# The first modulation's quarters on TensorE in the order first, third, second, fourth, and earlier loads of the next layer's scale quarters

## What is computed

```
mod = silu(c) @ w_ada[i] + b_ada[i]             # 1024 x 3072
sh, sc, gt = split(mod, 3)                      # shift, scale, gate: 1024 each
u = rms_norm(h, norm_g[i]) * (1 + sc) + sh
h = h + gt * mixer(u)
```

## Time and profile before

| | us |
|---|---|
| median of 3 runs | 1441.58 (1438.05 to 1445.44) |
| profiled execution | 1439.64 |
| its span | 1437.8 |
| TensorE busy | 1387.0 (96%) |
| VectorE busy | 749.6 (52%) |
| ACT, POOL busy | 578.9, 501.3 |
| mean granted TensorE clock | 0.972 of full |

### The profile page before, as it was taken

One profiled execution on the slowest core, in us unless ns is written; L12 is line 12 of the kernel. 1 busy time (PEld: TensorE's weight loads), 2 busy tenths in 40 slices (PEclk: granted clock), 3 DMA queues, 4 the chain that ended last, 5 costly groups with the idle time before them and its releaser, 6 DMA issues.

```text
span 1437.8 us, 18275 instructions
## 1 busy us (share of the span) xinstructions
PE 1387.0 (96%) x6981; PEld 1154.2 (80%) x6981; DVE 749.6 (52%) x1007; ACT 578.9 (40%) x892; POOL 501.3 (35%) x235
## 2 busy tenths in 40 slices
PE   7999999979999999999999999999999999999998
PEld 4688788769888888877879779788888888888886
DVE  3695888744845438477345425441635335253442
ACT  3444565514433344455444434443334223142331
POOL 0242000136531584311234213224475444444441
PEclk9999999989999999999999889989999999999999
DMA  9862001157322143211223113113333333333331
GB/s 344 270 216 68 3 19 30 30 174 231 97 76 57 57 133 103 74 44 45 76 60 88 45 44 88 44 51 96 102 88 103 89 102 95 95 102 88 101 97 65
DMA packets 204503, 136.20 MB, mean 95 GB/s; under 512 B 7033, under 2 KB 185834, under 8 KB 204442
## 3 DMA queue, kind: packets, MB, share of 16 engines
q1 hardware_dynamic: 204240, 135.32, 31.1%
q10 hardware_dynamic: 202, 0.06, 0.0%
HBM read 130.64 MB, written 4.72 MB: 94 GB/s over the span
## 4 chain that ended last, share of the span: by engine, by line
PE 83%; DVE 9%; ACT 3%; DMA 2%; issue 1%; POOL 1%; SPq 0%; ACTq 0%; DVEq 0%; POOLq 0%
PE psum L1972 26%; PE psum L1974 25%; PE psum L1973 25%; DMA ada_w<-in_w_ada 1%; PE psum L2020 1%; DVE pt_lo L1498 1%; PE psum L2169 1%; DMA ada_back<-in_w_ada 1%; DVE neg_max L1505 1%; POOL w_lo L642 1%; DVE psum L1448 1%; ACT w_hi L752 1%; PE psum L2410 1%; DVE probs L1493 1%; ACT pt_hi L898 1%
## 5 line engine op out<-in xcount | busy, mean ns | idle before, releaser
L642 POOL TENSOR_TENSOR w_lo<-w_raw,w_hi 128x1024 fp32r<-128x1024 f32 x180 | 439.7, 2446 | 745.6 <-ACT w_hi L752 617.5
L1972 PE MATMUL psum<-u_hi,w_hi 128*128 128x512 f32 (+1 forms) x960 | 373.3, 389 | 3.5 <-ACT decay_sum L1178 2.5
L1973 PE MATMUL psum<-u_lo,w_hi 128*128 128x512 f32 (+1 forms) x960 | 364.4, 380 | 0.0
L1974 PE MATMUL psum<-u_hi,w_lo 128*128 128x512 f32 (+1 forms) x960 | 364.1, 379 | 0.0
L752 ACT ACTIVATE w_hi<-w_raw 128x1024 fp32r<-128x1024 f32 x180 | 189.1, 1055 | 189.3 <-PE psum L1974 155.7
L1972 PEld LDWEIGHTS psum<-u_hi,w_hi 128*128 128x128 f32 x960 | 184.5, 192 | 42.9 <-issue 6.4
L1974 PEld LDWEIGHTS psum<-u_hi,w_lo 128*128 128x128 f32 x960 | 183.7, 191 | 34.0
L1973 PEld LDWEIGHTS psum<-u_lo,w_hi 128*128 128x128 f32 x960 | 184.3, 192 | 32.7 <-issue 1.4
L1972 PE MATMUL psum<-y_hi,w_hi 128*128 128x512 f32 x416 | 162.4, 390 | 0.0
L1973 PE MATMUL psum<-y_lo,w_hi 128*128 128x512 f32 x416 | 161.9, 389 | 0.0
L1974 PE MATMUL psum<-y_hi,w_lo 128*128 128x512 f32 x416 | 161.8, 389 | 0.0
(11 more groups left out here) (439 smaller groups left out, 2368.9 us busy)
## 6 DMA issues: line engine op xcount, KB each, us to landing
w_raw<-in_w_in SPq DMA_DIRECT2D x52, 512.0 KB, 3.8
ada_back<-in_w_ada SPq DMA_DIRECT2D x8, 2048.0 KB, 12.0
w_raw<-in_w_up SPq DMA_DIRECT2D x32, 512.0 KB, 4.0
w_raw<-in_w_down SPq DMA_DIRECT2D x32, 512.0 KB, 4.0
ada_w<-in_w_ada SPq DMA_DIRECT2D x4, 2048.0 KB, 14.8
w_raw<-in_fno_w_in SPq DMA_DIRECT2D x16, 512.0 KB, 3.7
w_raw<-in_mla_w_in SPq DMA_DIRECT2D x11, 512.0 KB, 4.8
w_raw<-in_mla_w_out SPq DMA_DIRECT2D x8, 512.0 KB, 4.1
```

The lines of the kernel that those rows point to most:

```text
L642: pool.tensor_tensor(WL[:, j, :], RAW[:, j % 2, :], f(WH[:, j, :]), ALU.subtract).then_inc(lo_done, 1)
L1972: pe.matmul(out, ah, bh, start=first, stop=False)
L1973: pe.matmul(out, ah, bl, start=False, stop=False)
L1974: return pe.matmul(out, al, bh, start=False, stop=last)
```

## The change

The four first quarters all go through TensorE, in the order 0, 2, 1, 3; their loads are queued as 0, 2, then the small bias tables, then 1, 3. VectorE's weighing of quarter 1, the selecting matmuls and eight warming matmuls go. The rstd diagonals and their matmuls come directly behind `ada(0)`. ACT splits weight tiles A0 0 and 1 behind the third row copy instead of behind the second. The fourth quarter's row is started behind `u0_lo` 3, since it shares a PSUM bank with a chunk of u.

Of the later quarters, r = 4 gets a buffer of its own (`AL4`, over the attention's finished latents); SyncE loads it once the last head's last scores are done, ahead of MO tile 4. Load 5 waits for the last weighing of values instead of the split output; load 6 follows MO tile 5 with no wait of its own, load 7 waits for `modulation(5)`. VectorE does `modulation(4)` in three pieces around the last head's end, and `modulation(5)` in two, behind output tiles 0 and 1. TensorE's sums of both move between half tiles 1 and 2.

```diff
+        AROW += [at("ada_row2", 166, [2, T]), at("ada_row3", 204, [2, T])]
+        AL4 = at("ada_late", 168, [P, KC, T])
...
-        ADA0 = 5
+        ADA0 = 6
-            return bank(2 if q == 3 else 6)
+            return bank(6 if q in (0, 3) else 2)
-            return AD[0] if r == 0 else AB[(r + 1) % 2]
+            return AD[0] if r == 0 else AL4 if r == 4 else AB[(r + 1) % 2]
@@ SyncE
             sp.dma_start(AQ[0][:], ada_weights(0)).then_inc(s_adaq[0], 16)
+            sp.dma_start(AQ[2][:], ada_weights(2)).then_inc(s_adaq[2], 16)
             sp.dma_start(T5[:], d["t5_bias_2"]).then_inc(s_t5, 16)
...
-            for q in range(1, 4):
+            for q in (1, 3):
                 sp.dma_start(AQ[q][:], ada_weights(q)).then_inc(s_adaq[q], 16)
...
-            for j in range(6):
+            for j in range(4):
                 out_tile(j)
-            sp.wait_ge(o_lo, HEADS)
+            sp.wait_ge(s_mm, 4 * HEADS)
             gate_load(4)
+            out_tile(4)
+            sp.wait_ge(un_mm, unit_mm_no(LAST, O_LAT))
             gate_load(5)
+            out_tile(5)
+            gate_load(6)
             out_tile(6)
             out_tile(7)
...
-            for r in range(6, 8):
-                sp.wait_ge(ada_used, r)
-                gate_load(r)
+            sp.wait_ge(ada_used, 6)
+            gate_load(7)
@@ ACT
             ada_row_copy(1, 2, 2)
-            split_hi(A0, None, 0)
-            split_hi(A0, None, 1)
...
             for c in range(4):
                 lat_hi(c)
-            ada_row_copy(2, 3, 4)
+            ada_row_copy(2, 1, 4)
+            split_hi(A0, None, 0)
+            split_hi(A0, None, 1)
+            ada_row_copy(3, 3, 5)
@@ VectorE
-            weigh_quarter(0)
             v.wait_ge(row_ss, TT + 1)
...
-            weigh_quarter(1).then_inc(ada_used, 1)
...
+            modulation(4, 0, 4)
             unit(LAST, O_LAT)
+            modulation(4, 4, 7)
             output(LAST)
             output_lo(LAST)
+            modulation(4, 7)
...
                 attention_added(c, bank(c), slice(0, T))
                 if c < 2:
-                    modulation(4 + c)
+                    modulation(5, 4 * c, 4 * c + 4)
@@ TensorE
+            pe.wait_ge(x_copied, KC)
             ada(0)
-            pe.wait_ge(bias_row, 1)
-            pe.wait_ge(x_copied, KC)
...
-            turn_row(0, 0)
-            for _ in range(8):
-                pe.matmul(bank(3, P), ONES[:], ONES[:], start=True, stop=True)
-            ada(2)
             pe.wait_ge(diag_done, TT)
...
+            turn_row(0, 0)
+            ada(2)
+            pe.wait_ge(bias_row, 1)
+            pe.matmul(bank(0), T5R[:], HOT[:, 0:T], start=True, stop=True)
+            pe.matmul(bank(1, P), T5R[:], HOT[:, T:TOEP], start=True, stop=True).then_inc(bias_mm, 1)
+            turn_row(1, 2).then_inc(ada_mm, 1)
+            ada(1)
+            pe.wait_ge(u0_lo, 3)
             ada(3, 0, 1)
-            turn_row(1, 2).then_inc(ada_mm, 1)
+            turn_row(2, 1)
             ada(3, 1, KC)
             def last_columns():
-                turn_row(2, 3)
...
+                turn_row(3, 3).then_inc(ada_mm, 1)
...
-            modulation(4)
-            modulation(5)
             for j in range(4):
                 pe.wait_ge(lo_done, MO + 4 + j + 1)
                 half_tile(0, j, j).then_inc(mo_half, 1)
+                if j == 1:
+                    modulation(4)
+                    modulation(5)
```

More of the change, by code:

```diff
@@ L190, in build @@
         DIAG = at("rstd_diag", 160, [P, TT, P])
-        SEL = at("two_columns", 155.875, [P, 2, 2])
         AROW = [at(f"ada_row{n}", 164 - 2 * n, [2, T]) for n in range(2)]
-        AROW.append(at("ada_row2", 166, [2, T]))
+        AROW += [at("ada_row2", 166, [2, T]), at("ada_row3", 204, [2, T])]
         XTOK = at("x_tok", 104, [P, TT, D])
@@ L544, in _ @@
             gate_tile(4)
-            sp.wait_ge(ada_used, 3)
+            sp.wait_ge(ada_used, 2)
             gate_load(3)
@@ L848, in head_hi @@
                 act.activation(WH[:, h % 4, 0:768], RAW[:, h % 2, 0:768], ACT.Copy).then_inc(hi_done, 1)
-            act.wait_ge(ada_used, 2)
+            act.wait_ge(ada_used, 1)
             for r in range(7):
@@ L1334, in _ @@
             v.memset(RSC[:], 0.0).then_inc(ones_set, 1)
-            link(v.memset(SEL[:], 1.0))
-            link(v.memset(SEL[:, 0, 1:2], 0.0))
-            v.memset(SEL[:, 1, 0:1], 0.0).then_inc(ones_set, 1)
             v.wait_ge(cols_t, 1)
@@ L1363, in _ @@
                 v.tensor_scalar(DIAG[:, m, :], IDENT[:], RSC[:, m:m + 1], None, ALU.mult).then_inc(diag_done, 1)
-            weigh_quarter(1).then_inc(ada_used, 1)
+            v.wait_ge(s_t5, 48)
+            v.tensor_copy(T5R[:].rearrange("b (h a) -> b h a", h=MH), T5[:].unsqueeze(2).to_broadcast([BUCKETS, MH, P // MH]))\
+                .then_inc(bias_row, 1)
             v.wait_ge(bias_mm, 1)
@@ L1435, in _, with modulation @@
             link(v.tensor_scalar(COLS[:, ROW["g_qa"]:ROW["g_qa"] + 2], COLS[:, ROW["g_qa"]:ROW["g_qa"] + 2], MLA_SCALE, None, ALU.mult))
[L1439 to L1443, removed]
+            def modulation(r, k0=0, k1=KC):
+                if k0 == 0:
+                    v.wait_ge(s_adaw[r % 2], 16 * (1 + r // 2 + 1))
+                    if r == 3:
+                        v.wait_ge(ada_mm, ADA0 + 1)
+                    if r:
+                        v.wait_ge(ada_used, r)
                 acc, w = ada_sum(r), ada_source(r)
                 part = acc if r >= 6 else bank(7 if r else 5)
[L1446 to L1449, removed]
+                for k in range(k0, k1):
+                    into = acc if k == KC - 1 else part
+                    if k:
+                        ins = v.scalar_tensor_tensor(into, w[:, k, :], CACT[:, k, 0:1], part, ALU.mult, ALU.add)
+                    else:
+                        ins = v.tensor_scalar(into, w[:, k, :], CACT[:, k, 0:1], None, ALU.mult)
+                    if k < KC - 1:
+                        link(ins)
+                    else:
+                        ins.then_inc(ada_used, 1)
             modulation(0)
@@ L1606, in _ @@
                 if c < 2:
-                    modulation(4 + c)
-            v.wait_ge(ada_mm, ADA0 + 6)
-            link(v.tensor_tensor(ADAL[1][:, 8:16], mod[:, 16:24, 0], COLS[:, b0 + 32:b0 + 40], ALU.add))
-            link(v.scalar_tensor_tensor(MULL[1][:], ADAL[1][:, 8:16], 1.0, COLS[:, g0 + 8:g0 + 16], ALU.add, ALU.mult))
+                    modulation(5, 4 * c, 4 * c + 4)
             for c in range(4, KC):
@@ L1613, in _ @@
                 attention_added(c, bank(c - 4, HALF), HALVES[0])
+                if c == 6:
+                    v.wait_ge(ada_mm, ADA0 + 6)
+                    link(v.tensor_tensor(ADAL[1][:, 8:16], mod[:, 16:24, 0], COLS[:, b0 + 32:b0 + 40], ALU.add))
+                    link(v.scalar_tensor_tensor(MULL[1][:], ADAL[1][:, 8:16], 1.0, COLS[:, g0 + 8:g0 + 16], ALU.add, ALU.mult))
             second_half(4)
@@ L2030, in _ @@
             pe.wait_ge(cact_done, 2)
+            pe.wait_ge(x_copied, KC)
             ada(0)
-            pe.wait_ge(bias_row, 1)
-            pe.wait_ge(x_copied, KC)
-            pe.matmul(bank(0), T5R[:], HOT[:, 0:T], start=True, stop=True)
-            pe.matmul(bank(1, P), T5R[:], HOT[:, T:TOEP], start=True, stop=True).then_inc(bias_mm, 1)
-            turn_row(0, 0)
-            for _ in range(8):
-                pe.matmul(bank(3, P), ONES[:], ONES[:], start=True, stop=True)
-            ada(2)
             pe.wait_ge(diag_done, TT)
@@ L2105, in modulation @@
             def modulation(r):
-                pe.wait_ge(ada_used, r + 2)
+                pe.wait_ge(ada_used, r + 1)
                 for b in range(4):
```

## The result

The changed kernel takes 1430.51 us (median of 7 runs, 1428.12 to 1434.51) against 1442.5 for the kernel before beside it: a ratio of 0.9921, 95% interval 0.9902 to 0.994. The forecast was 1428.5, range 1424.5 to 1434; the median lies 2.0 us above the forecast.

What follows compares the result with a forecast made beforehand. TensorE, busy 96% of the span, was taken as the bound. -11.9 behind the attention and +0.5 at the start sum to -11.4: 1428.2 from the profiled 1439.64, 1430.2 from the median; forecast 1428.5, range 1424.5 to 1434.

Steps and rivals of the forecast that it cites:

- Late part: Behind the attention: earlier loads and moved sums remove TensorE's waits and low-clock work before the half sums; 11.9 us less.
- Early part: At the start, first modulation's quarters all on TensorE: net +0.5 us, bounds -1.2 and +1.5.
- first term: At the start: VectorE's second half starts at 48.3 instead of 49.5, weight tile 2's low part at 60.1; 1.2 us less.
- second term: Before weight tile 2: TensorE waits 2.1 us and a low-clock stretch follows, costing 1.7 us.
- (1): Behind the attention: load 4 late by 5.4 us delays the O_LAT split; 3.3 us lost, about 1431.5; chance 0.10.
- (2): At half tile 1 or 3: VectorE stuck on load 5 delays add, square, split, POOL; 1431.5 to 1434; chance 0.07.
- (4): Behind the half tiles: Fourier weights' loads or POOL set the date, hiding the gain; 1436 to 1441; chance 0.05.
- (3): Before weight tile 2: no low clock behind the new idle time, whole early gain comes; 1426.5 to 1427; chance 0.25.
- (5): At the start: three quarters of two-column matmuls in a row lose the full clock; slower, 1448; chance 0.03.

Runs made afterwards that it cites:

- filled kernel: Kernel before with 12 and 25 extra 128-column matmuls on constants in TensorE's two idle times ahead of the sums: 1439.0 us, ratio 0.9998.
- the late load: Changed kernel with load 4 issued behind out_tile(4) instead of ahead of it: 1443.28 us, ratio 1.001.
- the fillers: Kernel before with 10 and 18 extra 128-column matmuls on constants in TensorE's two idle times ahead of the sums: 1441.34 us, ratio 0.9996.

## Why the prediction was right

**Size.** -11.4 was forecast against the profiled execution, -11.5 came; the medians differ by 12.0, and the ratio's interval stands for 9 to 14 us. The sum is right because the late part is. That the two profiled executions agree with it to 0.1 us is luck, as shown below. The step from there to 1428.5 took the profiled execution for typical; the median came at 1430.51, near the 1430.2 that the same sum gave from the median.

**Late part, -11.9: right.** Like with like the piece is 11.9 us shorter. Load 4 was issued at 277.8 (277.2 forecast) and took 8.0 us, less than the 9.2 of the nearest row. VectorE's operations on it took 0.78 us beside POOL's split, as priced. output(LAST) came at 292.69 (293.5 forecast), since in this execution turned() was 0.8 us early, without the low clock at 281; counted from the end of turned() it is 0.3 us later than before, as charged. Load 5 waited 2.65 us, within 2 to 4. The filled kernel confirms the low clock's share at 3.5 us, and k-steps of 0.36 us. The two profiles shown differ by 13.4 us in this piece, which is 11.9 and the low clock at 281.

**Early part, +0.5: the sign is right, its first term is wrong.** The step that failed is "1.2 us less". VectorE's second half started at 48.12 (48.3 forecast) and tile 2 at 59.89 (60.1), but the 61.30 that I subtracted from was that execution's own. Against the other kernels with the old order tile 2 starts 0.5 us later, and o_lat 0.8. The second term, +1.7 for the low clock behind the idle time near 60, took that idle time for the change's own; two of the kernels with the old early part have it as well. The clock fell behind it in three of five profiles of kernels with the new early part, in neither of those two, and not in the one shown. That the two terms add up to nearly what came (+0.8, and up to 1.7 more where the clock falls) is luck.

**What made the two profiled executions agree with the sum.** Up to o_lat the changed kernel lost 0.7 us (1.4 won at tile 2; then the low clock near 148, 1.7, and 0.4 more that I did not follow), it won 13.4 in the piece, and gave 1.2 back behind the half sums, where the low-clock stretches that both kernels have fall a little differently. From the half sums to the end kernels that wait for u_lo of the second norm for 1.0 us or less take 1097.7 to 1100.8: 3 us of play in any single execution.

**Rivals.** (1) and (2) are mechanisms that exist, each brought out by one late load, and (1)'s slope holds: a landing at 288.5 is 11.6 us behind before's o_lat matmul, the late load came 22.8 us behind its own, and TensorE waited 11.1 for the 11.2 between them. The piece grew by 12.9, the rest being what goes with the low clock behind the wait. (4) exists too, for a gain without the earlier loads. (3), no low clock behind the idle time near 60, is what the profiled execution did. It was a matter of chance and not the alternative I made of it: the idle times of 2.05 to 2.13 us near 60 were followed by the low clock in three of seven profiles. (5) is refuted: from 24 to 46, three quarters in a row, the granted clock was 1.00.

```profile
24.00:46.00 22.00, 22.00 (x60) 4.94 (x57) 6.66 (x13) 5.76 (x8) 4.65 (x2) 1.00 0.84 280
```

## What to carry to other kernels

Before a profiled time is used as a term, see whether it holds a low-clock stretch that the same work elsewhere does not have; a gain computed from it may be the execution's own. When a wait is removed, move what is queued behind it in the DMA queue as well: here moving the sums or filling the idle times won 4.4 and 3.5 us at the half sums without moving a load, neither kernel was faster, and in both TensorE waited for the next weight tile's chain (3.3 and 1.9 us). And where an engine's queue holds work for two consumers, put first the item that needs nothing (here ACT's split of a tile that had landed): that took 2 to 4 us off the kernel before, where the whole early part took off none.

## What the runs showed of the hardware

The granted clock falls to its 1.2 GHz level behind idle times of 1.6 to 2.5 us, but not each time. Behind the 1.98 to 1.99 us near 280, which all 14 profiles have, it fell in 10; behind 1.58 us near 148, which all have too, in 4; behind 2.08 to 2.67 us near 28 in one of six; behind 1.59 to 2.19 us near 15 in one of 14. One of 1.68 us, with the fillers ahead of it, was followed by 0.50. And it fell in four of seven profiles behind the 16 selecting matmuls of 2 columns, with no idle time of more than 0.1 us ahead of it. The Trainium skill (TensorE: Matmul & The Clock Gate, section "Why this matters for your kernels") warns only of longer gaps; these profiles disagree with it as a safe bound. The 2 MB loads took 7.8 to 8.1 us alone in the queue (load 4 in seven of the eight kernels that have the extra buffer), 9.7 beside other loads and, with another just ahead in the queue, 15.6 (before, issued at 299.08).
